# A mixture-of-experts layer: both transposes of the next pass's rows moved one chunk product earlier on TensorE

## The chip, the core and the metric

The kernel runs on one core of a Trainium2 chip. The metric is the device time of one execution, in microseconds (us), and a time is given as the median of several runs. The engines are TensorE (PE in the profile, with its weight loads as PEld), VectorE (DVE), ScalarE (ACT), GpSimd (POOL) and SyncE (SP), which here only issues DMA transfers. Each works through its own list of instructions in order and waits on semaphores that others raise.

## The reference

The layer takes 512 tokens of 1024 numbers. A mixing stage (differential attention, retention, an output projection) comes first; then each token goes to 4 of 32 experts, and their outputs are weighted, added and normalized. The change touches only the expert stage:

```
logits = (x2d @ w_router) + b_router
top_val, top_idx = lax.top_k(logits, TOP_K)          # 4 of 32
gates = softmax(top_val)
for each block of 128 rows that belong to one expert e:
    h = xb @ w_in[e] + b_in[e]                       # 1024 -> 2048
    glu = minimum(h[:, ::2], 7);  lin = clip(h[:, 1::2], -7, 7)
    act = glu * sigmoid(1.702 * glu) * (lin + 1)
    y = act @ w_out[e] + b_out[e]                    # 1024 -> 1024
x = x + sum over the 4 experts of gate * y
out = rms_norm(x, norm_f_g)
```

Everything is float32.

## The kernel before, in words

**Passes.** The expert stage is a loop over passes. A pass takes up to 128 token rows that go to the same expert, and streams this expert's weights from memory: 8 chunks of 1 MB of the first matrix and 4 of the second, 12 a pass. With these inputs there are 33 passes (the down projection's 132 loads are 4 a pass), so 396 chunks. Pass 0 is written out, passes 1 to 32 run in a hardware loop, and the down projection of the last pass stands behind it.

**Chunks.** To reach float32 accuracy with TensorE's faster float32 mode, each chunk is split in two: ScalarE rounds it (`make_hi`, L1037) and VectorE computes the remainder (`make_lo`, L1436). Both have three buffers. TensorE then does 12 matmuls of 128x512 for the chunk (`product`): 4 pairs at L801 and L803 on the rounded part, and 4 at L809 on the remainder, after which it raises `chunk_used`. So `make_hi` of a chunk waits until the chunk three before it is used, and `make_lo` waits for `make_hi`. The raw chunks land in a ring of six slots; SyncE issues a load when both halves of the chunk six before it have been made.

**One pass on TensorE.** I number the chunks of a pass 0 to 11: 0 to 3 are `up(p, 0, 0..3)`, the first half of the expert's columns; 4 to 7 are `down` of the pass before; 8 to 11 are `up(p, 1, 0..3)`, the second half. Between them stand small products: the bias (L816), transposes of the activations (`act_transposes`, L827), the list of the next pass's tokens (`token_list`, L768), and the transposes of the next pass's input rows (`x_transposes`, L776, in two halves, here called half 0 and half 1).

**How the next pass's rows come.** TensorE's token list is read by VectorE (`read_list`, L1428 to L1431) behind `make_lo` of chunk 7. GpSimd then gathers the 128 rows of 4 KB by index (`gather`, L1634). TensorE waits for them at half 0 of `x_transposes`, half 1 follows, and ScalarE and VectorE turn each half into rounded part and remainder (`x_hi`, L1043; `x_lo`, L1441), between the splits of the following chunks. The order on ScalarE at the turn of a pass is: chunk 11, `x_hi` 0, chunk 0, chunk 1, `x_hi` 1, chunk 2, a sigmoid, chunk 3, chunk 4. VectorE has: chunk 11, `x_lo` 0, chunk 0, chunk 1, `x_lo` 1, chunk 2, the activation (L1448 to L1452), chunk 3, and so on up to chunk 7 and `read_list`. The lines

```
if a == 1 and not (isinstance(p, int) and p == 0):
    act.wait_ge(chunk_used, Step(p, 0).number)
```

in `x_hi` make half 1 wait until TensorE has used all chunks of the pass before, because chunks 10 and 11 read the tile that it writes. GpSimd also scatters the finished rows of the pass before (`scatter`, L1641), some microseconds after the gather, on the same queue.

**What sets the order.** Each engine's order is written out by hand in its `one_pass`; nothing is scheduled automatically.

Of the kernel before, what the change touches and what calls it, by code (L numbers as in the profile page):

```python
# [107 lines left out]
def build(nc, x, positions, norm1_g, w_in, lambda_q1, lambda_k1, lambda_q2, lambda_k2, diff_norm_g,  # L108
# [3 lines left out]
    with ctx:  # L112
# [426 lines left out]
        def _(pe):  # L539
# [232 lines left out]
            def x_transposes(p, a):  # L772
                if a == 0:
                    pe.wait_ge(gathered, 16 * (p + 1))
                for k in range(KH):
                    mm = pe.transpose(bank[6 + a][:, k * P:(k + 1) * P],  # L776
                                      x_rows[:, (a * KH + k) * P:(a * KH + k + 1) * P], ident)
                mm.then_inc(x_transposed, 1)
# [16 lines left out]
            def product(p, j, dst, k0, left_hi, left_lo, start, stop):  # L795
                c = Step(p, j)
                pe.wait_ge(hi_made, c.number + 1)
                for k in range(2):
                    for f in range(2):
                        cols = slice(f * 512, (f + 1) * 512)  # L800
                        pe.matmul(dst[:, f, :], left_hi[:, k0 + k, :], hi[c.buffer][:, k, cols],  # L801
                                  start=(start and k == 0), stop=False)
                        pe.matmul(dst[:, f, :], left_lo[:, k0 + k, :], hi[c.buffer][:, k, cols],  # L803
                                  start=False, stop=False)
                pe.wait_ge(lo_made, c.number + 1)
                for k in range(2):
                    for f in range(2):
                        cols = slice(f * 512, (f + 1) * 512)
                        mm = pe.matmul(dst[:, f, :], left_hi[:, k0 + k, :], lo[c.buffer][:, k, cols],  # L809
                                       start=False, stop=(stop and k == 1))  # L810
                mm.then_inc(chunk_used, 1)

            def bias_of_half(g):
                for f in range(2):
                    at_f = (2 * g + f) * 512
                    pe.matmul(pair[g][:, f, :], pick_bias, b_in_parts[:, at_f:at_f + 512], start=True, stop=False)  # L816

            def up(p, g, k):
                product(p, g * SECOND + k, pair[g], 2 * k, xT_hi, xT_lo, False, k == QUARTERS - 1)
# [4 lines left out]
            def act_transposes(p, g):  # L824
                pe.wait_ge(act_ready, p * 2 + (g + 1))
                for n in range(4):
                    mm = pe.transpose(bank[7][:, n * P:(n + 1) * P], act_rows[:, g, n * P:(n + 1) * P], ident)  # L827
                mm.then_inc(act_transposed, 1)
# [15 lines left out]
            def second_half(p, before):  # L844
                if before:
                    pe.wait_ge(half_read, p * 2)
                bias_of_half(1)
                up(p, 1, 0)
                act_transposes(p, 0)
                up(p, 1, 1)  # L850
                up(p, 1, 2)
                pe.wait_ge(idx_ready, p + 2)
                x_transposes(p + 1, 0)
                up(p, 1, 3)
                pe.wait_ge(actT_lo_made, p * 2 + 1)
                x_transposes(p + 1, 1)

            def one_pass(p):
                first_half(p, True)
                pe.wait_ge(down_banks_free, p)  # L860
                pe.wait_ge(actT_lo_made, p * 2 - 1)
                down(p, DOWN, 0)
                token_list(p + 1)
                down(p, DOWN + 1, 1)
                pe.wait_ge(actT_lo_made, p * 2)
                down(p, DOWN + 2, 2)
                down(p, DOWN + 3, 3)
                second_half(p, True)

            first_half(0, False)  # L870
            token_list(1)
            second_half(0, False)
            by_pass(pe, one_pass)
            done = after_last(pe)
# [837 lines left out]
```

## Time and profile before

| what | value |
|---|---|
| median of 3 runs | 1689.02 us (1685.94 to 1689.54) |
| the profiled execution | 1689.54 us, of which the span (first to last instruction) is 1687.7 us |
| busy share of the span | PE 91%, DVE 78%, ACT 59%, POOL 28% |
| mean granted TensorE clock | 0.958 of full speed |
| moved by DMA | 476.45 MB, mean 282 GB/s |
| chain that ended last, by engine | DVE 32%, PE 21%, DMA 20%, issue 19%, ACT 6% |

The table is from the page of the profile, a summary of one execution. The rows below come from that page and from questions to the same trace: the list of waits (which instruction stood idle, for whom, how long in all and how often), the timeline (start and length of each instruction, and in brackets the idle time before it and who ended it), one line's instructions, and stretches of time with each engine's busy time and the granted TensorE clock. A matmul's end is modelled, and neighbouring matmuls overlap, so a matmul that starts 0.23 us after the last is listed with 0.40 us.

### The profile page before, as it was taken

The page shows a single profiled execution, that of the slowest core. Times are in us where ns is not written, and L with a number is a line of the kernel's source. Part 1 is how long each engine was busy: PE and PEld are TensorE (multiplying, and loading weights), DVE is VectorE, ACT ScalarE, POOL GpSimd, SP SyncE. Part 2 cuts the span into 40 slices and gives each one's busy share as a digit, 9 for nine tenths or more (in the row PEclk, how much of TensorE's full clock was granted, in tenths as well). Part 3 has the DMA queues.
Part 4 walks back from the last instruction along what each step waited for, and adds up shares of the span by engine and source line. Part 5 has one row for each costly group of instructions (what it writes and reads, how often), then busy time and mean ns, then how long its engine had stood idle before and what let it go on. Part 6 is the DMA issues. An engine that isn't in the chain of part 4 may idle for free.

```text
span 1687.7 us, 23889 instructions
## 1 busy us (share of the span) xinstructions
PE 1542.2 (91%) x7535; PEld 1250.5 (74%) x7535; DVE 1312.1 (78%) x1260; ACT 996.5 (59%) x897; POOL 464.3 (28%) x376
## 2 busy tenths in 40 slices
PE   2999687968999999999999999999999999999982
PEld 2999556746877777777777777777777777777762
DVE  3542662356889998888999988988988898988886
ACT  4221441214777766767777667667777677667752
POOL 0000312001133333333332233333333333333322
PEclk9999887967999999999999999999999999999996
DMA  7210601006899999999999999999999999999984
GB/s 254 94 33 1 249 1 38 19 37 225 319 353 352 347 354 349 348 351 360 359 352 357 356 350 346 360 346 363 348 354 345 350 358 345 355 356 365 348 325 169
DMA packets 141836, 476.45 MB, mean 282 GB/s; under 512 B 12784, under 2 KB 29808, under 8 KB 141744
## 3 DMA queue, kind: packets, MB, share of 16 engines
q1 hardware_dynamic: 128096, 445.23, 73.1%
q0 software_dynamic: 10128, 28.06, 4.6%
q10 hardware_dynamic: 3584, 2.78, 0.5%
q8 instruction: 18, 0.29, 0.1%
q14 instruction: 10, 0.08, 0.0%
HBM read 463.45 MB, written 21.50 MB: 287 GB/s over the span
## 4 chain that ended last, share of the span: by engine, by line
DVE 32%; PE 21%; DMA 20%; issue 19%; ACT 6%; ACTq 1%; DVEq 1%; SPq 0%; POOLq 0%; POOL 0%
DVE split L1436 20%; DMA work<-h_rows,token_next 18%; ACT split L1037 4%; PE pair L693 4%; PE pair L560 3%; PE pair L564 3%; PE pair L559 3%; DVE work L1449 2%; DVE work L1448 2%; DVE operands L1420 1%; PE pair L776 1%; PE pair L801 1%; DVE operands L1457 1%; PE pair L803 1%; PE pair L809 1%
## 5 line engine op out<-in xcount | busy, mean ns | idle before, releaser
L1436 DVE TENSOR_TENSOR split<-ring,split 128x2048 fp32r<-128x2048 f32 x396 | 893.9, 2284 | 44.7 <-ACT split L1037 44.7
L1037 ACT CAST split<-ring 128x2048 fp32r<-128x2048 f32 x396 | 754.2, 1913 | 200.0 <-PE pair L809 195.3
L801 PE MATMUL pair<-split,operands 128*128 128x512 f32 x1584 | 639.4, 404 | 7.9 <-issue 7.9
L803 PE MATMUL pair<-split,operands 128*128 128x512 f32 x1584 | 628.8, 397 | 0.0
L809 PE MATMUL pair<-split,operands 128*128 128x512 f32 x1584 | 438.7, 398 | 0.0
L809 PEld LDWEIGHTS pair<-split,operands 128*128 128x128 f32 x1584 | 296.3, 189 | 81.4 <-DVE split L1436 11.6
L801 PEld LDWEIGHTS pair<-split,operands 128*128 128x128 f32 x1584 | 299.2, 189 | 74.5 <-issue 8.2
L803 PEld LDWEIGHTS pair<-split,operands 128*128 128x128 f32 x1584 | 299.7, 189 | 67.3
L1634 POOL DMA_INDIRECT work<-h_rows,token_next x34 | 76.7, 2255 | 585.0 <-DVE token_next L1431 580.0
L1043 ACT CAST operands<-pair 128x512 fp32r<-128x512 f32 x66 | 38.7, 587 | 170.4 <-PE pair L776 170.4
L1441 DVE TENSOR_TENSOR operands<-pair,operands 128x512 fp32r<-128x512 f32 x66 | 45.4, 687 | 93.2 <-ACT operands L1043 93.1
L1641 POOL DMA_INDIRECT expert_rows<-work,dest_cur x33 | 95.1, 2883 | 74.4 <-PE pair L809 53.3
L559 PE MATMUL pair<-split,operands 128*128 128x256 f32 x384 | 95.0, 281 | 4.2 <-issue 4.2
L560 PE MATMUL pair<-split,operands 128*128 128x256 f32 x384 | 95.3, 286 | 0.0
L1647 POOL CAST dest_cur<-list_mid 128x1 int32<-128x1 f32 x33 | 44.0, 1333 | 161.7 <-DMA expert_rows<-work,dest_cur 161.7
L559 PEld LDWEIGHTS pair<-split,operands 128*128 128x128 f32 x384 | 73.3, 191 | 4.4 <-issue 4.4
L560 PEld LDWEIGHTS pair<-split,operands 128*128 128x128 f32 x384 | 72.7, 189 | 0.0
L1197 DVE COPY work<-pair 128x256 f32<-128x256 f32 x24 | 10.2, 425 | 79.3 <-PE pair L564 79.3
L776 PE MATMUL pair<-cst,work 128*128 128x128 f32 x272 | 43.3, 283 | 26.2 <-DMA work<-h_rows,token_next 26.0
L776 PEld LDWEIGHTS pair<-cst,work 128*128 128x128 f32 x272 | 31.8, 142 | 46.2 <-DMA work<-h_rows,token_next 35.0
L1627 POOL CAST operands<-work 64x128 fp32r x34 | 65.2, 1917 | 0.0
L693 PE MATMUL pair<-late_ring,work 128*128 128x256 f32 x256 | 59.4, 395 | 4.6 <-issue 2.9
(210 smaller groups left out, 1383.8 us busy)
## 6 DMA issues: line engine op xcount, KB each, us to landing
ring<-in_w_moe_in SPq DMA_DIRECT2D x264, 1024.0 KB, 7.2
ring<-in_w_moe_out SPq DMA_DIRECT2D x132, 1024.0 KB, 8.3
ring<-in_w_in SPq DMA_DIRECT2D x12, 1024.0 KB, 9.6
ring<-expert_rows SPq DMA_DIRECT2D x3, 2048.0 KB, 8.4
late_ring<-in_w_o SPq DMA_DIRECT2D x4, 1024.0 KB, 9.7
resid<-in_x SPq DMA_DIRECT2D x4, 512.0 KB, 6.3
h_rows<-work ACTq DMA_DIRECT2D x4, 512.0 KB, 2.7
late_ring<-expert_rows SPq DMA_DIRECT2D x4, 512.0 KB, 5.3
```

Source lines behind the costliest of these rows:

```text
L559: pe.matmul(dst, hT_hi[:, k, at_i], w_hi[s][:, k, :], start=(k == 0), stop=False)
L560: pe.matmul(dst, hT_lo[:, k, at_i], w_hi[s][:, k, :], start=False, stop=False)
L693: mm = pe.matmul(dst, mixT[:, i % 2, k, :], slot(s)[:, k, :], start=(k == 0), stop=(k == KT - 1))
L776: mm = pe.transpose(bank[6 + a][:, k * P:(k + 1) * P], x_rows[:, (a * KH + k) * P:(a * KH + k + 1) * P], ident)
L801: pe.matmul(dst[:, f, :], left_hi[:, k0 + k, :], hi[c.buffer][:, k, cols], start=(start and k == 0), stop=False)
L803: pe.matmul(dst[:, f, :], left_lo[:, k0 + k, :], hi[c.buffer][:, k, cols], start=False, stop=False)
L809: mm = pe.matmul(dst[:, f, :], left_hi[:, k0 + k, :], lo[c.buffer][:, k, cols], start=False, stop=(stop and k == 1))
L1037: act.copy(hi[c.buffer], raw[c.slot]).then_inc(hi_made, 1)
L1436: dve.tensor_tensor(lo[c.buffer], raw[c.slot], hi[c.buffer].bitcast(F32), ALU.subtract).then_inc(lo_made, 1)
L1627: pool.tensor_copy(pick_bias[0:2 * NE, :], col(expert_rows, e).to_broadcast([2 * NE, SLOTS]))\
L1634: pool.indirect_dma_start(out=x_rows, out_offset=None, in_=h2_dram, in_offset=bass.IndirectOffsetOnAxis(ap=token_next[:, 0:1], axis=0))\
L1641: pool.indirect_dma_start(out=y_dram, in_=y_rows, in_offset=None, out_offset=bass.IndirectOffsetOnAxis(ap=dest_cur[:, 0:1], axis=0), bound ...
```

## The change

In `second_half`, which ends every pass on TensorE, both halves of `x_transposes` for the next pass move ahead of one chunk product each. Before, the order was chunk 9, chunk 10, half 0, chunk 11, half 1; now it is chunk 9, half 0, chunk 10, half 1, chunk 11. The two waits in front of the halves move with them. Nothing is added or removed, and the order on the other four engines is the same as before.

```diff
                 up(p, 1, 0)
                 act_transposes(p, 0)
                 up(p, 1, 1)
-                up(p, 1, 2)
                 pe.wait_ge(idx_ready, p + 2)
                 x_transposes(p + 1, 0)
-                up(p, 1, 3)
+                up(p, 1, 2)
                 pe.wait_ge(actT_lo_made, p * 2 + 1)
                 x_transposes(p + 1, 1)
+                up(p, 1, 3)
```

On TensorE, inside the loop, the 12 matmuls of chunk 10 (one L801/L803 pair per step, then four L809 at once) leave their place in front of half 0 (L774, L776), where the engine waits for the gathered rows:

```order
-L797 REGISTER_ALU
-L801 MATMUL pair<-split,operands 128x512 [waits hi_made]
-L803 MATMUL pair<-split,operands 128x512
-L801 MATMUL pair<-split,operands 128x512
-L803 MATMUL pair<-split,operands 128x512
-L801 MATMUL pair<-split,operands 128x512
-L803 MATMUL pair<-split,operands 128x512
-L801 MATMUL pair<-split,operands 128x512
-L803 MATMUL pair<-split,operands 128x512
-L809 MATMUL pair<-split,operands 128x512 [waits lo_made]
-L809 MATMUL pair<-split,operands 128x512 x3
 L774 REGISTER_ALU [waits idx_ready]
```

So the wait for the rows is reached one chunk product sooner. At the end of the loop's body, behind half 1 (L776), a chunk product now stands in front of the branch (L436) that leads to the next pass:

```order
 L776 MATMUL pair<-cst,work 128x128 x3
+L797 REGISTER_ALU
+L801 MATMUL pair<-split,operands 128x512 [waits hi_made]
+L803 MATMUL pair<-split,operands 128x512
+L801 MATMUL pair<-split,operands 128x512
+L803 MATMUL pair<-split,operands 128x512
+L801 MATMUL pair<-split,operands 128x512
+L803 MATMUL pair<-split,operands 128x512
+L801 MATMUL pair<-split,operands 128x512
+L803 MATMUL pair<-split,operands 128x512
+L809 MATMUL pair<-split,operands 128x512 [waits lo_made]
+L809 MATMUL pair<-split,operands 128x512 x3
```

Behind half 0 there are now two chunk products to the end of the pass, 10 and 11, where there was one.

## Rows read from the trace of the kernel before

**Rows 1.** The page, busy us, share of the span, count.

```profile
PE 1542.2 (91%) x7535; PEld 1250.5 (74%) x7535; DVE 1312.1 (78%) x1260; ACT 996.5 (59%) x897; POOL 464.3 (28%) x376
```

**Rows 2.** Waits: engine, line, who ended it, us in all, times, longest.

```profile
POOL work L1634 <- DVE token_next L1431: 580.0, 33, 30.7
...
PE pair L776 <- DMA work<-h_rows,token_next: 26.0, 30, 4.7
```

**Rows 3.** Timeline of PE, one pass: start us, length us, instruction.

```profile
797.74 0.66 PE L776 MATMUL pair<-cst,work 128*128 128x128 f32 x4 [0.88 <-DMA work<-h_rows,token_next]
798.15 0.48 PE L801 MATMUL pair<-split,operands 128*128 128x512 f32 x1
...
800.10 1.09 PE L809 MATMUL pair<-split,operands 128*128 128x512 f32 x4
801.03 0.60 PE L776 MATMUL pair<-cst,work 128*128 128x128 f32 x4
801.38 0.71 PE L816 MATMUL pair<-operands 128*128 128x512 f32 x2
...
815.44 1.09 PE L809 MATMUL pair<-split,operands 128*128 128x512 f32 x4
```

**Rows 4.** Timeline of ACT in the same pass.

```profile
798.92 3.72 ACT L1037 CAST split<-ring 128x2048 fp32r<-128x2048 f32 x2
802.53 0.59 ACT L1043 CAST operands<-pair 128x512 fp32r<-128x512 f32 x1
803.01 1.93 ACT L1037 CAST split<-ring 128x2048 fp32r<-128x2048 f32 x1
...
816.57 1.91 ACT L1037 CAST split<-ring 128x2048 fp32r<-128x2048 f32 x1 [0.34 <-PE pair L809]
```

**Rows 5.** Timeline of DVE in the same pass.

```profile
800.86 4.49 DVE L1436 TENSOR_TENSOR split<-ring,split 128x2048 fp32r<-128x2048 f32 x2 [1.12 <-ACT split L1037]
...
805.88 2.28 DVE L1436 TENSOR_TENSOR split<-ring,split 128x2048 fp32r<-128x2048 f32 x1
...
822.07 2.28 DVE L1436 TENSOR_TENSOR split<-ring,split 128x2048 fp32r<-128x2048 f32 x1
...
824.53 0.16 DVE L1431 CAST token_next<-pair 128x1 int32<-128x1 f32 x1
```

**Rows 6.** Timeline of POOL: the first gather under load, then the same pass.

```profile
408.69 2.29 POOL L1634 DMA_INDIRECT work<-h_rows,token_next  x1 [26.66 <-DVE token_next L1431]
...
825.56 2.29 POOL L1634 DMA_INDIRECT work<-h_rows,token_next  x1 [16.59 <-DVE token_next L1431]
829.47 2.75 POOL L1641 DMA_INDIRECT expert_rows<-work,dest_cur  x1 [1.62 <-PE pair L809]
```

**Rows 7.** Timeline of PE: half 0 at the first and at the last gather.

```profile
418.53 0.63 PE L776 MATMUL pair<-cst,work 128*128 128x128 f32 x4 [4.67 <-DMA work<-h_rows,token_next]
...
1630.38 0.66 PE L776 MATMUL pair<-cst,work 128*128 128x128 f32 x4 [0.27 <-DMA work<-h_rows,token_next]
```

**Rows 8.** Line 1634, all 34 gathers.

```profile
DMA to landing us min/median/max: 4.5/10.0/10.6
```

**Rows 9.** Timeline of PE behind the last pass.

```profile
1633.68 0.60 PE L776 MATMUL pair<-cst,work 128*128 128x128 f32 x4
1642.21 0.79 PE L801 MATMUL pair<-split,operands 128*128 128x512 f32 x1 [7.94 <-issue]
...
1647.49 0.77 PE L827 MATMUL pair<-cst,work 128*128 128x128 f32 x4
```

**Rows 10.** Stretches: length, busy us of PE, PEld, DVE, ACT, POOL; PEclk; DMA; GB/s.

```profile
420.00:425.00 5.00, 5.00 (x21) 3.97 (x20) 3.89 (x3) 4.34 (x4) 0.00 (x0) 0.76 0.03 11
985.00:990.00 5.00, 3.68 (x20) 3.01 (x20) 1.17 (x2) 2.90 (x3) 0.72 (x3) 1.00 1.03 415
1640.00:1645.00 5.00, 2.79 (x7) 2.24 (x8) 3.92 (x4) 0.00 (x0) 0.00 (x0) 0.50 1.01 384
```

**Rows 11.** Timeline of PE: half 0 with the longest gather.

```profile
986.40 0.66 PE L776 MATMUL pair<-cst,work 128*128 128x128 f32 x4 [1.32 <-DMA work<-h_rows,token_next]
```

## The prediction, made before the changed kernel was run

> **What bounds the kernel now.** The page first: TensorE is busy 91% of the span [rows 1], so it looks like the bound. The list of waits says otherwise. At half 0 of the row transposes TensorE stands idle for the gathered rows in 30 passes, 26.0 us in all, 4.7 us the longest; GpSimd in turn waits 580.0 us for VectorE's token index [rows 2], and VectorE works on what follows from those same transposes. That is a closed ring from pass to pass, so I followed one pass in the timelines, counting time from the start of half 0 (t = 0, at 797.74 us).
>
> The ring is: rows landed, half 0 on TensorE, `x_hi` 0 and the split of chunk 0 on ScalarE, then VectorE, whose first `make_lo` starts at t = 3.12 (800.86) [rows 5]. From there VectorE's timeline has no idle entry until the token index at t = 26.79 (824.53) [rows 5]. The gather starts at t = 27.82 (825.56) [rows 6], and lands a median of 10.0 us later [rows 8]; then half 0 of the next pass starts and the ring closes. 27.82 + 10.0 = 37.82 us a pass. The check: half 0 after the first loaded gather starts at 418.53, the last at 1630.38 [rows 7], and 1211.85 / 32 passes = 37.87 us. So the loop's time is this ring, and the mean gather by it is 37.87 - 27.82 = 10.05 us. TensorE comes second and close: of the 26.0 us of waits 4.7 belong to the gather before the first of these 32 passes, so it waits 21.3 / 32 = 0.67 us a pass and would need 37.20 us by itself.
>
> **The change, part by part.** It moves two groups of instructions on one engine, and adds no work. What counts is which products TensorE now does between the landing and the things that ScalarE waits for.
>
> 1. Reaching half 0 sooner. TensorE gets there one product, 2.88 us (798.15 to 801.03) [rows 3], earlier in its list. But half 0 starts when the rows have landed, and in a loop that is closed by the gather TensorE's work per pass stays 37.20 us wherever the wait stands in it. So this neither gains nor costs: the wait just absorbs the difference between the ring and 37.20. In the very first gather, where TensorE already waits 4.67 us [rows 7], it waits longer and half 0 starts as before.
>
> 2. Chunk 10 behind half 0. It starts at t = 0.41 as chunk 11 did (798.15) and its last matmuls end at t = 3.45 (800.10 + 1.09) less t = 0 at 797.74 [rows 3]. ScalarE's split of chunk 1 needs the buffer of chunk 10. A split that waits for TensorE starts 0.04 us after the modelled end: 816.57 after 815.44 + 1.09 [rows 3, 4]. So chunk 1 is rounded from t = 3.49 to 5.42. VectorE's two splits take 4.49 us together and 2.28 alone, so it took that of chunk 1 at t = 3.12 + 2.21 = 5.33 [rows 5]; now 5.44, and it is through at 7.65, well ahead of what step 3 gives for the next.
>
> 3. Chunk 11 behind half 1. Half 1 starts at t = 3.29 as now (801.03) [rows 3], its operands have long been there. 0.35 us later (801.03 to 801.38 in rows 3) chunk 11 starts, at t = 3.64, and ends 3.04 us after its start (798.15 to 801.19), at t = 6.68. Before, it ended at 3.45. Two things on ScalarE need it: `x_hi` 1, by the lines quoted above, and the split of chunk 2, whose buffer it frees. `x_hi` 1 therefore starts at t = 6.72; today it starts at 4.79 (802.53). The split of chunk 2 follows 0.48 us later as now (802.53 to 803.01) [rows 4], at t = 7.20, and ends at 9.13 (1.93 us). VectorE starts 0.02 us after that (800.86 against 798.92 + 1.92), at t = 9.15. Today its `make_lo` of chunk 2 starts at t = 8.14 (805.88) [rows 5]. **VectorE is 1.01 us late**, on the ring, and has no idle time behind it up to the token index that could take this back.
>
> 4. Is anything later than that? Chunk 0's products come behind the bias: that starts at t = 3.64 + 2.88 = 6.52 where it was 3.64 (801.38), so every product up to chunk 9 is 2.88 us later against the landing. The last split that matters for the token index is chunk 7's: at t = 18.83 + 2.88 = 21.71, done at 23.62 (816.57, 1.91 us) [rows 4]. VectorE takes chunk 7 at t = 24.33 + 1.01 = 25.34 (822.07) [rows 5]. 1.7 us to spare, so the price stays 1.01 and doesn't grow to 2.88.
>
> 5. The gather itself and the ring of raw chunks. No instruction of VectorE, GpSimd or SyncE changes place, and the gather is issued behind the same VectorE work, so I keep 10.05 us. The scatter, 3.91 us behind the gather today (829.47) [rows 6], waits for TensorE and comes nearly 2 us later (2.88 - 1.01). The nearest row for a gather without a scatter behind it is the first loaded one, 408.69 to 418.53 = 9.84 us [rows 6, 7]: at most 0.2 us a pass, 7 us in all. From the other side the gathers lie up to 10.6 us [rows 8], 0.55 more a pass, 18 us. The loads come 3% slower than today, which speaks for the lower side if for any. I take no change.
>
> 6. Behind the last pass. TensorE's body now ends with chunk 11 (t = 6.68) where it ended with half 1, at t = 3.90 (1633.68 + 0.60 against 1630.38) [rows 7, 9]. Then come 7.94 us in which it waits for nothing that the profile shows, the loop's way out, and the last down projection. If these start when the body's last instruction is done, they are 2.8 us later; if TensorE's sequencer goes through them while chunk 11 runs, nothing. I take 2.8.
>
> The sum: 32 passes x 1.01 = 32.3, plus 2.8 = 35.1 us. The profiled execution took 1689.54 us; 1689.54 + 35.1 = 1724.6. It lies 0.5 us above the median of the runs, so for that the forecast is 1724 us, 2.1% slower. The wait at half 0 then is 37.87 + 1.01 - 37.20 = 1.68 us a pass.
>
> On the gather the Trainium skill gives another price. Its page "DMA: Bandwidth & Descriptors" (Anatomy of one DMA) fits a GpSimd transfer as 2.0 us plus its bytes over 436 GB/s, an estimate of 3.2 us for 512 KB; this case's median is 10.0 us under the weight loads [rows 8]. By the fit the ring would be 27.82 + 3.2, far below TensorE's own 37.20, and the change would cost nothing but the end of the kernel. The trace decides for 10.0.
>
> **The rivals.**
>
> (a) The price is hidden: within 0.2%. VectorE's late second would vanish if the gather came 1 us sooner, in 9.05 us. For it: the scatter goes out of its way, the loads are a little thinner, and the unloaded gather took 4.5 us [rows 8]. Against: the loaded gather without a scatter took 9.84. It gives 1689 to 1692 us.
>
> (b) Faster. The mechanism is the same transfer: if spreading gather and scatter apart makes the gather shorter by more than 1.01 us, the ring falls below today's, down to TensorE's 37.20 us, where it stops. The point from which it decides is a gather of 9.04 us. At the floor it gives 32 x 0.67 = 21.4 us less, 2.8 more at the end: 1671 us. Against it stands the same 9.84.
>
> (c) TensorE's place counts fully. If some split before the token index had no slack, the 2.88 us of step 4 would be on the ring: 32 x 2.88 = 92 us, 1784 us with the end. For it: it takes only 1.7 us of slack that I have read from one pass. Against: the slack comes from VectorE's own unbroken work, which is alike in each pass.
>
> (d) The TensorE clock. A wait of 1.7 us a pass might let it fall. A wait of 1.32 us left it at 1.00, that is 2.4 GHz [rows 10, 11]; after the 4.67 us wait it was 0.76 on average, and after 7.94 us idle 0.50, 1.2 GHz [rows 7, 9, 10]. One product at the low clock took 5.28 us (1642.21 to 1647.49) instead of 2.80, and with one slow product behind each landing that is 32 x 2.48 = 79 us more: 1804 us. The row of 1.32 us lies nearer to 1.68 than that of 4.67.
> The Trainium skill, "TensorE: Matmul & The Clock Gate" (Part 1: The HAM clock gate), says that the slow clock is the state at rest and that activity holds the fast one, so longer idling speaks for (d); the trace agrees for its two long gaps and shows nothing between.
>
> **How the numbers follow.** A difference under about 0.2% (3.4 us) can't be told from no change. The forecast of about 1 us a pass has 0.70; its own range is 0.5 to 1.4 us a pass, 1706 to 1737 us (16 and 45 us, plus the end). A smaller loss, with the gather making up more than half, has 0.06; (a) 0.08; (b) 0.07; (c) 0.05; (d) 0.04. Slower is the sum of four of these, 0.85; the same 0.08; faster 0.07. For 8 times in 10 the range takes the forecast's own and the smaller loss down to 1702, and up to 1738.
>
> **What would show it.** Right: the start of half 0 to the start of the next gather is 28.83 us instead of 27.82; `make_lo` of chunk 2 starts near t = 9.15 behind an idle entry of about 0.9 us that ends on ScalarE's split, new in VectorE's list of waits (some 30 us over the kernel); `x_hi` 1 starts at 6.7; TensorE's waits for the rows sum to about 32 x 1.7 + 7.5 = 61 us; the clock in the loop stays 1.00. Step 5 is right if the median gather stays at 10.0. I am wrong if the gather's median falls below 9.1, if VectorE shows further idle entries before the token index, or if TensorE's clock falls in the passes.

## The result and the profile after

The changed kernel takes 1744.88 us (median of 4 runs, 1737.98 to 1756.62) against 1689.28 us before, measured beside it: a ratio of 1.0337 (95% interval 1.0276 to 1.0399), 3.4% slower. The forecast was 1724 us, 2.1% slower, with a range of 1702 to 1738; the direction is right and the size is not. The profiled execution of the changed kernel took 1740.34 us (span 1738.5), 50.8 us more than that of before.

| | before | after |
|---|---|---|
| span, us | 1687.7 | 1738.5 |
| PE, DVE busy | 91%, 78% | 89%, 76% |
| mean granted TensorE clock | 0.958 | 0.948 |
| TensorE's waits for the rows, us | 26.0 | 69.2 |

The list of waits after the change (us in all, times, longest), which answers to [rows 2]:

```profile
POOL work L1634 <- DVE token_next L1431: 702.7, 33, 33.7
...
DVE split L1436 <- ACT split L1037: 125.2, 114, 6.1
...
ACT operands L1043 <- PE pair L809: 42.4, 32, 1.3
...
PE pair L776 <- DMA work<-h_rows,token_next: 69.2, 33, 7.5
```

ScalarE's `x_hi` (L1043) now waits 32 times for a chunk product (L809), a wait that the list of before does not have. VectorE's wait for ScalarE's split has grown from 44.7 us to 125.2, by far more than the forecast's 30 or so. Read by its place in the pass, 26.3 us of the growth is the forecast entry in front of chunk 2 (32 times, 0.82 each), 19.6 stands in front of chunk 1 in 14 passes, which the second pass below explains, and 34.5 in front of chunk 11, behind the token index, where it is not on the ring. The gather itself did not change (line 1634, all gathers; before: 10.0 the median, [rows 8]):

```profile
DMA to landing us min/median/max: 4.4/9.9/10.8
```

**A pass as forecast.** Timeline of TensorE, then ScalarE, then VectorE of the changed kernel, from half 0 at 846.37:

```profile
846.37 0.66 PE L776 MATMUL pair<-cst,work 128*128 128x128 f32 x4 [1.15 <-DMA work<-h_rows,token_next]
846.78 0.48 PE L801 MATMUL pair<-split,operands 128*128 128x512 f32 x1
...
849.66 0.60 PE L776 MATMUL pair<-cst,work 128*128 128x128 f32 x4
...
851.97 1.09 PE L809 MATMUL pair<-split,operands 128*128 128x512 f32 x4
```

```profile
853.10 0.59 ACT L1043 CAST operands<-pair 128x512 fp32r<-128x512 f32 x1 [1.32 <-PE pair L809]
853.58 1.91 ACT L1037 CAST split<-ring 128x2048 fp32r<-128x2048 f32 x1
```

```profile
855.52 2.29 DVE L1436 TENSOR_TENSOR split<-ring,split 128x2048 fp32r<-128x2048 f32 x1 [0.82 <-ACT split L1037]
```

Half 1 starts 3.29 us behind half 0. Chunk 11 ends at t = 6.69 (851.97 + 1.09), `x_hi` 1 starts at 6.73 and VectorE takes chunk 2 at 9.15, after 0.82 us of idle time that was not there. The next gather starts at 875.22, 28.85 us after half 0, where it was 27.82.

**A pass that was not forecast.** The same order, TensorE from half 0 at 1042.15:

```profile
1042.15 0.82 PE L776 MATMUL pair<-cst,work 128*128 128x128 f32 x4 [1.86 <-DMA work<-h_rows,token_next]
1042.62 0.78 PE L801 MATMUL pair<-split,operands 128*128 128x512 f32 x1
...
1043.62 0.63 PE L801 MATMUL pair<-split,operands 128*128 128x512 f32 x1
...
1046.07 1.09 PE L809 MATMUL pair<-split,operands 128*128 128x512 f32 x4
1047.00 0.60 PE L776 MATMUL pair<-cst,work 128*128 128x128 f32 x4
```

VectorE in the same pass, the split of chunk 1, which needs chunk 10 done:

```profile
1049.14 2.29 DVE L1436 TENSOR_TENSOR split<-ring,split 128x2048 fp32r<-128x2048 f32 x1 [1.43 <-ACT split L1037]
```

The stretches of the changed kernel around it, and last a like stretch of the pass from 1003.35, which ran at full clock (length, busy times, clock, DMA share, GB/s):

```profile
1040.00:1042.00 2.00, 0.29 (x2) 0.00 (x0) 2.00 (x1) 0.00 (x0) 0.00 (x0) 1.00 1.03 375
1042.20:1045.60 3.40, 3.40 (x11) 2.82 (x12) 0.91 (x3) 2.38 (x2) 0.00 (x0) 0.55 1.03 388
1046.00:1048.00 2.00, 2.00 (x12) 1.64 (x12) 1.71 (x1) 0.80 (x1) 0.92 (x2) 1.00 1.02 418
1003.40:1007.00 3.60, 3.60 (x21) 3.01 (x21) 1.22 (x2) 2.56 (x3) 0.64 (x3) 1.00 1.03 418
```

Behind a wait of 1.86 us the granted clock is 0.55 for 3.4 us, near its lower level of 1.2 GHz, and back at 1.00 when chunk 10's last four matmuls run. Chunk 10 ends at t = 5.01 instead of 3.45, and VectorE takes chunk 1 at 6.99, behind 1.43 us of idle time. Half 1 comes 4.85 us behind half 0 instead of 3.29, and the next gather (1072.56) 30.41 us behind it instead of 28.85.

I read half 0 and the next gather in all 32 passes of both traces. Before, the distance is 27.8 us in each. After, it is 28.85 us in 18 passes and 30.1 to 30.7 in 14 (30.40 on average). The gathers average 10.06 us before and 10.02 after. In the first pass the clock falls in both kernels (half 1 comes 4.81 us behind half 0 before, 5.15 after), but only with two products behind the rows does that reach the ring (27.78 us before, 30.71 after). So the loop's 53.8 us are 32 x 1.04 = 33.3 for the longer road behind the rows, 14 x 1.55 = 21.7 for the fallen clock, and -1.2 for the gathers. The rest of the span is 1.8 us more from the last half 0 to the end (59.1 against 57.3), and 4.8 us less before the first loaded half 0 (413.76 against 418.53), which is there already at the first half 0 of all (381.40 against 386.43), ahead of everything that the edit moves; the first loaded half 0 lies between 412.5 and 418.5 in the other traces too. 53.8 + 1.8 - 4.8 = 50.8.

### The profile page after: what moved, and what is told of

It reads as the page before. It is cut to its first block, busy times and chain, and to the rows that moved or that the text cites. A ratio compares the mean times of both kernels' runs of the same rounds, so it can differ in the third digit from the quotient of the medians.

```text
span 1738.5 us, 23889 instructions
## 1 busy us (share of the span) xinstructions
PE 1551.9 (89%) x7535; PEld 1265.9 (73%) x7535; DVE 1327.1 (76%) x1260; ACT 1006.6 (58%) x897; POOL 307.0 (18%) x376
## 4 chain that ended last, share of the span: by engine, by line
PE 32%; DVE 26%; DMA 19%; issue 15%; ACT 6%; ACTq 1%; DVEq 1%; POOLq 0%; SPq 0%; POOL 0%
DMA work<-h_rows,token_next 18%; DVE split L1436 15%; PE pair L801 5%; PE pair L803 5%; PE pair L809 4%; ACT split L1037 4%; PE pair L693 3%; PE pair L559 3%; PE pair L564 3%; PE pair L560 3%; DVE work L1448 2%; DVE work L1449 2%; PE pair L776 2%; DVE operands L1457 1%; DMA expert_rows<-work,dest_cur 1%
## 5 line engine op out<-in xcount | busy, mean ns | idle before, releaser
L1436 DVE TENSOR_TENSOR split<-ring,split 128x2048 fp32r<-128x2048 f32 x396 | 900.9, 2289 | 126.4 <-ACT split L1037 125.2
L801 PE MATMUL pair<-split,operands 128*128 128x512 f32 x1584 | 653.6, 413 | 7.7 <-issue 7.7
L803 PE MATMUL pair<-split,operands 128*128 128x512 f32 x1584 | 637.5, 402 | 0.0
L809 PE MATMUL pair<-split,operands 128*128 128x512 f32 x1584 | 436.8, 397 | 0.0
L801 PEld LDWEIGHTS pair<-split,operands 128*128 128x128 f32 x1584 | 305.5, 193 | 74.5 <-issue 8.1
L809 PEld LDWEIGHTS pair<-split,operands 128*128 128x128 f32 x1584 | 301.1, 190 | 74.3
L803 PEld LDWEIGHTS pair<-split,operands 128*128 128x128 f32 x1584 | 305.8, 193 | 66.7
L1043 ACT CAST operands<-pair 128x512 fp32r<-128x512 f32 x66 | 38.7, 587 | 167.7 <-PE pair L776 125.2
L776 PE MATMUL pair<-cst,work 128*128 128x128 f32 x272 | 45.9, 296 | 69.2 <-DMA work<-h_rows,token_next 69.2
L776 PEld LDWEIGHTS pair<-cst,work 128*128 128x128 f32 x272 | 33.2, 148 | 89.5 <-DMA work<-h_rows,token_next 75.6
L559 PEld LDWEIGHTS pair<-split,operands 128*128 128x128 f32 x384 | 73.1, 190 | 7.6 <-issue 7.6
L560 PEld LDWEIGHTS pair<-split,operands 128*128 128x128 f32 x384 | 73.9, 192 | 0.0
L1641 POOL DMA_INDIRECT expert_rows<-work,dest_cur x33 | 50.7, 1536 | 125.6 <-PE pair L809 101.3
L1647 POOL CAST dest_cur<-list_mid 128x1 int32<-128x1 f32 x33 | 33.6, 1018 | 216.5 <-DMA expert_rows<-work,dest_cur 216.5
L693 PEld LDWEIGHTS pair<-late_ring,work 128*128 128x128 f32 x256 | 51.2, 202 | 13.4 <-issue 3.7
## 6 DMA issues: line engine op xcount, KB each, us to landing
ring<-in_w_in SPq DMA_DIRECT2D x12, 1024.0 KB, 10.9
```

The source lines that it names most:

```text
L559: pe.matmul(dst, hT_hi[:, k, at_i], w_hi[s][:, k, :], start=(k == 0), stop=False)
L560: pe.matmul(dst, hT_lo[:, k, at_i], w_hi[s][:, k, :], start=False, stop=False)
L693: mm = pe.matmul(dst, mixT[:, i % 2, k, :], slot(s)[:, k, :], start=(k == 0), stop=(k == KT - 1))
L776: mm = pe.transpose(bank[6 + a][:, k * P:(k + 1) * P], x_rows[:, (a * KH + k) * P:(a * KH + k + 1) * P], ident)
L1436: dve.tensor_tensor(lo[c.buffer], raw[c.slot], hi[c.buffer].bitcast(F32), ALU.subtract).then_inc(lo_made, 1)
L1641: pool.indirect_dma_start(out=y_dram, in_=y_rows, in_offset=None, out_offset=bass.IndirectOffsetOnAxis(ap=dest_cur[:, 0:1], axis=0), bound ...
```

## The experiments

Theories at the start: **A**, the pass is closed by the gather, and each product between the landed rows and the end of chunk 11 counts; **C**, on top of it the clock falls behind the longer wait. Ratios are to the kernel before, measured on the same chip (1687.12 us for e1 to e4, 1687.39 for e5 to e7). The diffs of e1, e2, e4, e6 and e7 are against the kernel before, that of e3 against the changed kernel; those of e1, e2 and e6 leave out the waits in front of the two halves, which stay with them.

### e1: only half 0 moved

```diff
 up(p, 1, 1)
-up(p, 1, 2)
 x_transposes(p + 1, 0)
+up(p, 1, 2)
 up(p, 1, 3)
 x_transposes(p + 1, 1)
```

> Order on TensorE: chunk 9, half 0, chunk 10, chunk 11, half 1: only half 0 is moved, half 1 stays last. Theory A (the pass is closed by the gather, and what costs is that two chunk products, not one, stand between the landed rows and the end of chunk 11): chunk 11 ends at t = 6.3, half 1 at 6.8, so ScalarE's second half of the rows starts at about 6.8 as in the changed kernel (6.7), half 0 to the next gather is 28.9 to 29.0 us in passes at full clock; 30.4 to 30.6 where the clock has fallen behind the wait. Time within 0.5% of the changed kernel, 1730 to 1755 us. Rival B (moving half 1 ahead of chunk 11 costs, by its own wait or its place): near the kernel before, 1690 us.

Measured: 1752.32 us, ratio 1.0398 (1.0371 to 1.0425), slower as the changed kernel is. In its trace 18 passes have 28.9 us from half 0 to the next gather and 14 have 30.5 (the first of them 31.0). At full clock the second half of the rows starts at t = 6.80 on ScalarE (half 0 is at 653.18):

```profile
659.98 0.59 ACT L1043 CAST operands<-pair 128x512 fp32r<-128x512 f32 x1 [1.39 <-PE pair L776]
```

In e1 it waits for half 1 (L776), in the changed kernel for chunk 11, and it starts at nearly the same time (6.80 and 6.73): it is the two products behind the rows that cost. B falls.

### e2: only half 1 moved

```diff
 up(p, 1, 2)
 x_transposes(p + 1, 0)
-up(p, 1, 3)
 x_transposes(p + 1, 1)
+up(p, 1, 3)
```

> Order: chunk 9, chunk 10, half 0, half 1, chunk 11: only half 1 is moved. Theory A: one chunk product stands behind the landed rows as before; chunk 11 ends at t = 3.8 instead of 3.45, before ScalarE is through with chunk 1 (4.8), so half 0 to the next gather stays 27.8 us, TensorE waits about 0.7 us a pass, the clock stays 1.00: the time of the kernel before, 1687 to 1691 us. Rival B: the loss shows here, some 20 to 50 us.

Measured: 1689.32 us, ratio 1.0019 (0.9999 to 1.0040; 10 runs against 13): no difference that can be told. Half 0 to the next gather is 27.8 us in every pass behind the first (28.45 there), and the waits for the rows are as before:

```profile
PE pair L776 <- DMA work<-h_rows,token_next: 24.9, 31, 3.6
```

So of the change's two moves that of half 0 carries the whole loss.

### e3: the wait filled

The changed kernel with work in place of most of its wait:

```diff
 pe.wait_ge(idx_ready, p + 2)
+for n in range(12):
+    pe.transpose(bank[6][:, (n % 4) * P:(n % 4 + 1) * P], ident, ident)
 x_transposes(p + 1, 0)
```

> The changed kernel with 12 spare 128x128 transposes of the identity in front of half 0 (some 1.05 us of TensorE work in the place of its wait); they write a bank that half 0 overwrites. Theory C (on top of 1.04 us a pass, the TensorE clock falls behind a wait of about 2 us in 14 of 32 passes of the profiled run and costs 1.54 us in each): with the idle time cut to under 1.3 us the clock stays 1.00 in the loop, half 0 to the next gather is 28.85 us in all passes, half 1 is 3.29 us behind half 0 in all, and the time is 1724 us plus or minus 4, 1% under the changed kernel. Rival D (the long passes come from the transfers or the splits, and the low clock only goes with them): the long passes stay, 1738 us or more.

Measured: 1723.56 us, ratio 1.0212 (1.0182 to 1.0242). Adding 12 transposes to each pass took 21 us away from the changed kernel's median (1744.88, ratio 1.0337; the two intervals do not touch), and left the time that the forecast had without the clock. A pass of it (L853 is the filling), and a stretch around it:

```profile
806.08 1.47 PE L853 MATMUL pair<-cst 128*128 128x128 f32 x12
808.74 0.65 PE L776 MATMUL pair<-cst,work 128*128 128x128 f32 x4 [1.19 <-DMA work<-h_rows,token_next]
...
812.03 0.60 PE L776 MATMUL pair<-cst,work 128*128 128x128 f32 x4
```

```profile
806.00:812.00 6.00, 4.81 (x30) 3.94 (x28) 3.04 (x3) 2.39 (x2) 0.02 (x1) 1.00 1.02 411
```

```profile
PE pair L776 <- DMA work<-h_rows,token_next: 25.3, 29, 5.1
```

The clock is 1.00 over 500 to 1600 us; half 0 to the gather is 28.85 us in all passes but the first, whose wait is still 5.07 us and whose clock falls (31.15). C stands, D falls.

### e4: the token list read earlier, TensorE's order as before

```diff
 make_lo(p, 6)
+read_list(p + 1)
 swiglu(p, 0)
 make_lo(p, 7)
-read_list(p + 1)
```

> The kernel before with VectorE's reading of the token list moved ahead of the activation and of the split of chunk 7, about 4.0 us earlier in its order; TensorE's order as before. Theory A: the gather's ring needs 33.9 us, so TensorE's own 37.2 us a pass is what is left; it waits for no rows any more; 32 x 0.67 = 21 us less, 1668 us plus or minus 4. Rival E (the loop is held by VectorE or by the DMA queues as such): no change, 1689 us.

Measured: 1669.02 us, ratio 0.9901 (0.9876 to 0.9925), 1% faster. TensorE waits for the rows once, ahead of the loop's first pass, and what little it waits for in the loop is the remainder of chunk 7, with the 0.4 us of the list now ahead of it on VectorE:

```profile
891.15 1.20 PE L809 MATMUL pair<-split,operands 128*128 128x512 f32 x4 [0.28 <-DVE split L1436]
```

A pass takes 37.27 us, near the 37.20 that [rows 2, 7] gave for TensorE alone. E falls.

### e5: the same edit in the changed kernel

> The changed kernel with the same edit on VectorE as e4 (token list read ahead of the activation and of the split of chunk 7). Theory A: with the rows there before TensorE comes, no wait is left in front of half 0, so neither the late second half of the rows (1.04 us) nor the fallen clock has anything to act on: TensorE's own 37.3 us a pass, the time of e4 plus at most 2.8 us at the end, 1669 to 1674 us, 4% under the changed kernel, and clock 1.00 in the loop. Rival F (the order of the change costs by itself, through the later splits): 1 us a pass or more stays over e4, 1700 us or more.

Measured: 1657.15 us, ratio 0.9800 (0.9761 to 0.9840): 5% under the changed kernel and the fastest of all. No wait for the rows is left in the loop, and TensorE is busy without a gap; the stretch of 400 us inside the loop of e5, and the same of e4:

```profile
700.00:1100.00 400.00, 400.00 (x1829) 324.28 (x1829) 370.16 (x284) 292.75 (x207) 84.09 (x110) 1.00 0.99 364
```

```profile
700.00:1100.00 400.00, 397.05 (x1803) 318.84 (x1802) 361.44 (x281) 285.33 (x204) 127.07 (x110) 1.00 0.98 360
```

F falls, and my own 1669 to 1674 missed too, on the slow side. A pass takes 36.75 us here and 37.27 in e4. In e4 TensorE comes to the remainder of chunk 7 before VectorE has it; the last four matmuls of that chunk start 3.25 us behind those of chunk 6 (891.15 against 887.90). In e5 they start 2.80 us behind:

```profile
888.27 1.10 PE L809 MATMUL pair<-split,operands 128*128 128x512 f32 x4
891.07 1.10 PE L809 MATMUL pair<-split,operands 128*128 128x512 f32 x4
```

That is 0.45 of the 0.52 us. Half 0 one product sooner gives ScalarE and VectorE the rows sooner against TensorE's list. It is a gain of the very order that loses above, once the rows no longer end the pass.

### e6: half 0 and half 1 behind chunk 11

```diff
 up(p, 1, 2)
+up(p, 1, 3)
 x_transposes(p + 1, 0)
-up(p, 1, 3)
 x_transposes(p + 1, 1)
```

> The opposite move in the kernel before: chunk 9, 10, 11, half 0, half 1; VectorE as before. Theory A by the same count: nothing stands between the rows and chunk 0, so TensorE waits there for the first half of the rows (ready 2.0 us behind half 0) and for chunk 0's remainder (5.3 us behind half 0), some 2.6 us a pass that it can't make up, since it has to do chunk 11 ahead of half 0 as well: about 39.3 to 39.8 us a pass, some 1735 to 1750 us, with TensorE's waits at chunk 0 and not at half 0. Rival G (the later the transposes the better, since fewer products stand behind the rows): 1689 us or less.

Measured: 1744.31 us, ratio 1.0336 (1.0294 to 1.0378), 39.74 us a pass: inside both ranges. TensorE no longer waits for the rows but for the first split of the new pass:

```profile
1048.43 1.04 PE L776 MATMUL pair<-cst,work 128*128 128x128 f32 x8
1049.23 0.71 PE L816 MATMUL pair<-operands 128*128 128x512 f32 x2
1051.51 0.49 PE L801 MATMUL pair<-split,operands 128*128 128x512 f32 x1 [1.57 <-ACT split L1037]
```

G falls. With the list where it was, the kernel before had half 0 at the best of the three places tried: a product earlier costs on the ring of the gather; a product later, TensorE waits 1.57 us a pass for the rows' first split (50.2 us in 32 waits) and some tenths more behind it.

### e7: the token list read later, TensorE's order as before

```diff
 make_lo(p, 7)
-read_list(p + 1)
-for j in range(8, 11):
+make_lo(p, 8)
+read_list(p + 1)
+for j in range(9, 11):
     make_lo(p, j)
```

> The kernel before with the token list read one split later on VectorE (behind chunk 8's instead of chunk 7's), 2.2 us later. TensorE's order as before. Theory A: the whole 2.2 us is on the ring, 30.0 us from half 0 to the gather, 40.1 us a pass, TensorE waits 2.9 us a pass. Theory C: behind waits of that length the clock falls in most passes, with this order too; but here only chunk 11 stands between the rows and its end, which then comes at t = 4.9 to 5.1 instead of 3.45, hardly later than ScalarE is ready (4.8), so a fallen clock costs 0.3 us a pass at most, not 1.54. Together 1689 + 70 to 80 = 1757 to 1769 us. Rival H (the clock falls only with the changed order, for another reason than the wait): clock 1.00 in the loop.

Measured: 1797.31 us, ratio 1.0640 (1.0600 to 1.0680). The clock falls with the order of before as well, behind the longer waits:

```profile
825.87 0.66 PE L776 MATMUL pair<-cst,work 128*128 128x128 f32 x4 [2.93 <-DMA work<-h_rows,token_next]
826.29 0.66 PE L801 MATMUL pair<-split,operands 128*128 128x512 f32 x1
...
827.17 0.63 PE L801 MATMUL pair<-split,operands 128*128 128x512 f32 x1
...
830.71 0.60 PE L776 MATMUL pair<-cst,work 128*128 128x128 f32 x4
```

H falls, and half 0 to the next gather is 30.0 us in most passes though the clock fell in them, as expected: with one product behind the rows the low clock has next to no price (the mean is 30.18 us, and seven passes have 30.5 to 31.0). But the total is 28 us over the upper end of my range. A pass takes 41.1 us, of which the ring is 30.2 and the gather 10.94 (10.06 before):

```profile
DMA to landing us min/median/max: 4.5/10.9/11.4
```

0.88 us x 32 = 28 us, which is the miss. Its cause is open: the scatter follows the gather by 3.04 us instead of 3.91, and the loads beside it are at another place, and no run separates the two. The shorter gathers of e4 and e5 (medians 8.5 and 8.3 us, counted from the start of GpSimd's instruction) have for the most part another reason, which the traces show. Before and after the change GpSimd starts each loaded gather while VectorE is at a split, and its instruction takes 2.25 to 2.31 us. In e4 and e5 it starts during the activation, and takes 1.02 to 1.07 in 32 gathers of 33; the one that starts during a split takes 2.29 and 2.28. Of e4:

```profile
887.41 0.68 DVE L1449 SCALAR_TENSOR_TENSOR work<-pair,work 128x512 f32<-128x512 f32 x1
```

```profile
887.77 1.06 POOL L1634 DMA_INDIRECT work<-h_rows,token_next  x1 [12.39 <-DVE token_next L1431]
```

That is 1.2 us of the 1.5 and 1.7.

## Why the prediction was wrong

**What bounds the kernel**: right. The ring of the gather, TensorE second. e4 took the ring away and the loop settled at 37.27 us a pass. But 37.20 was not TensorE's own need. The list of waits counts from modelled ends, and before the change it leaves out a short wait for chunk 7's remainder, which starts 2.92 us behind that of chunk 6 where 2.80 is the step without a wait:

```profile
821.49 1.09 PE L809 MATMUL pair<-split,operands 128*128 128x512 f32 x4
...
824.41 1.20 PE L809 MATMUL pair<-split,operands 128*128 128x512 f32 x4
```

e5, in which TensorE is never idle in the loop, puts its need at 36.75. No term of the forecast's sum rested on it; the floor of rival (b), the forecast of the wait and my expectation for e5 did.

**Step 2, chunk 10, and step 3, chunk 11**: right in place and size. Forecast 1.01 us a pass with `x_hi` 1 at t = 6.72 and chunk 2 at 9.15; measured 1.04, 6.73 and 9.15. e1 and e2 show that it is half 0's place alone, and e3 shows the whole of it at full clock: 1723.56 us.

**Step 4, nothing later**: right, 28.85 us and not 2.88 more.

**Step 5, the gather unchanged**: right, 10.02 us against 10.05, with the scatter moved.

**Step 6, the end**: 1.8 us instead of 2.8. The last down projection starts 2.5 us later behind half 0 (14.35 us against 11.83), and the clock, low behind both ways out of the loop, came back sooner in its first product.

**Step 1 is the one that failed.** It put the longer wait at nothing: reaching half 0 sooner "neither gains nor costs: the wait just absorbs the difference between the ring and 37.20". The runs show 21.7 us in its place. The mean wait was forecast as 1.68 us a pass and came out at 1.93 ((69.2 - 7.5) / 32); single waits lay between 0.85 and 2.80. But the idling was not free here: in 14 passes TensorE's clock fell (one of them the first, behind the wait of 7.5 us), and the product that paid was chunk 10, on the ring. I had this mechanism as rival (d) and argued it away, since the row with 1.32 us of wait lay nearer to the mean of 1.68 than the row with 4.67. That compared a mean with two single rows. A longest gather of 10.6 us against a median of 10.0 [rows 8] already meant single waits of 2.3 us, and between 1.32 and 4.67 no row said what the clock does. The rival's price was too high per pass (2.48 us; measured 1.55, because the clock was back before the chunk's last four matmuls) and it struck 14 passes, not 32: 21.7 us in place of 79.

The median lies 4.5 us above the profiled execution, and the five executions of the changed kernel differ by 19 us, those of before by 6. The longest has the lowest mean clock (0.939 at a span of 1754.8 us, 0.947 and 0.948 at 1736.2 and 1738.5). That fits more or fewer passes with a fallen clock, but it is read from five means, not from their passes.

## What to carry to other kernels

In a loop whose pass is closed by a transfer, what matters is not how early an engine reaches its wait, but how much work stands between the landing and the next thing that the ring needs: of two orders with the same work, the one with less behind the landing wins, as long as it leaves the engine other work until the rows are converted (e6 had nothing behind the landing, and lost 3.4% as well). Moving the request itself earlier (e4, e5) wins more and can turn the verdict on the order. Before calling slack on TensorE free, set the longest single waits, not the mean, beside the rows that show its clock holding or falling. An order that was tuned around one bound should be tried again once this bound is gone.

## What the runs showed of the hardware

- In the trace of the changed kernel TensorE's granted clock fell behind waits of 1.86 us and held behind others of 1.94 and 2.30 us, so length alone doesn't decide there. It fell behind each wait from 2.40 us up and behind none below 1.86; in e1 it held behind one of 2.51. Spare work in place of idling made the kernel faster (e3, 1723.56 us against 1744.88).
- The gather of 512 KB under a steady stream of weight loads took a median of 8.3 us (e5) to 10.9 us (e7), and 4.5 us in pass 0, ahead of that stream [rows 8]. GpSimd's part of it took 2.25 to 2.31 us when it started during one of VectorE's splits and 1.02 to 1.07 during the activation's L1449.
- GpSimd was busy 464.3 us before and 307.0 after with the same 376 instructions. The same pattern shows there: the cast at L1627 took 2.06 to 2.09 us in 31 passes before, each time beside one of VectorE's splits, and 0.31 to 0.36 after, where VectorE was idle. It is not on the path in either.
